# Feed-forward output stages: 12 of 22 inner k tiles by seven block products in place of eight

## The reference

```
def swiglu(x, w_in, w_out):                      # w_in 1024 x 5632, w_out 2816 x 1024
    gate, up = jnp.split(x @ w_in, 2, axis=-1)
    return (jax.nn.silu(gate) * up) @ w_out
x <- LN1(alpha*x + 0.5*swiglu_1(x))              # stages f1i (input), f1o (output)
x <- LN2(alpha*x + W_out[concat(PoolMix(u), RWKV7(z))])   # stages z, wo
h  = alpha*x + 0.5*swiglu_2(x)                   # stages f2i, f2o
x <- LN3(h + sigmoid(h W_g + b_g) * (p W_ple))   # stage gp
```

## Time and profile before

| | us |
|---|---|
| median of 3 runs (2641.80 to 2646.03) | 2642.49 |
| span of the profiled execution (the page shows no time around it) | 2641.4 |
| PE busy | 2536.3 (96%) |
| DVE / ACT / POOL busy | 1686.9 / 933.7 / 1585.4 |
| matmuls | 27280 |
| read from and written to HBM | 186.95 MB, 3.12 MB |

### The profile page before, as it was taken

How to read it: one execution, slowest core, us unless ns; L and a number is a source line. 1 busy time by engine, 2 the same in 40 slices (tenths; PEclk the granted TensorE clock), 3 DMA queues, 4 the chain that set the end, 5 groups by cost and what they waited for, 6 DMA issues and landing times. The chain is left out here.

```text
span 2641.4 us, 65842 instructions
## 1 busy us (share of the span) xinstructions
PE 2536.3 (96%) x27280; PEld 2444.1 (93%) x27280; DVE 1686.9 (64%) x2492; ACT 933.7 (35%) x1942; POOL 1585.4 (60%) x1319
## 2 busy tenths in 40 slices
PE   8999999989999999999999999999899999999997
PEld 8999999978888999999999999999788799999996
DVE  5866318756663889931598982377566659898124
ACT  3444004445531345410245530144445214553002
POOL 6555666734325677666767766667343266776665
PEclk9999999999998999999999999999899999999998
DMA  4222332200001232223222323321000022332322
GB/s 155 96 98 81 91 105 73 81 2 5 4 21 42 81 104 98 94 84 95 86 96 98 103 85 88 96 81 57 4 4 5 20 73 89 102 102 82 88 87 79
DMA packets 81901, 193.70 MB, mean 73 GB/s; under 512 B 13680, under 2 KB 14064, under 8 KB 81648
## 3 DMA queue, kind: packets, MB, share of 16 engines
q1 hardware_dynamic: 78192, 187.07, 22.1%
q10 hardware_dynamic: 3456, 3.02, 0.4%
HBM read 186.95 MB, written 3.12 MB: 72 GB/s over the span
## 5 line engine op out<-in xcount | busy, mean ns | idle before, releaser
L874 PE MATMUL ps<-xa,w_hi 128*128 128x272 f32 x2208 | 583.4, 289 | 4.2 <-DVE w_lo L1800 2.7
L874 PE MATMUL ps<-xa,w_lo 128*128 128x272 f32 x1932 | 560.6, 290 | 0.0
L874 PE MATMUL ps<-xb,w_hi 128*128 128x272 f32 x1656 | 478.9, 289 | 0.0
L665 POOL TENSOR_SCALAR w_hi<-w_raw 128x1024 fp32r<-128x1024 f32 (+2 forms) x217 | 232.0, 1069 | 366.0 <-PE ps L760 359.0
L874 PEld LDWEIGHTS ps<-xa,w_hi 128*128 128x128 f32 x2208 | 399.2, 189 | 6.5 <-DVE w_lo L1800 3.3
L874 PEld LDWEIGHTS ps<-xa,w_lo 128*128 128x128 f32 x1932 | 364.2, 189 | 0.0
L669 POOL TENSOR_TENSOR w_lo<-w_raw,w_hi 128x640 fp32r<-128x640 f32 (+2 forms) x217 | 352.1, 1623 | 0.0
L874 PEld LDWEIGHTS ps<-xb,w_hi 128*128 128x128 f32 x1656 | 312.7, 189 | 0.0
L760 PE MATMUL ps<-hh,w_hi 128*128 128x272 f32 x1472 | 304.9, 288 | 5.6 <-DVE hl L1828 5.4
L760 PE MATMUL ps<-hh,w_lo 128*128 128x272 f32 x1472 | 302.7, 288 | 0.0
L760 PE MATMUL ps<-hl,w_hi 128*128 128x272 f32 x1472 | 302.3, 287 | 0.0
(11 more groups left out here) (364 smaller groups left out, 5698.2 us busy)
## 6 DMA issues: line engine op xcount, KB each, us to landing
w_raw<-in_wz SPq DMA_DIRECT2D x44, 512.0 KB, 3.3
w_odd<-in_w1i SPq DMA_DIRECT2D x72, 256.0 KB, 3.0
w_odd<-in_w2i SPq DMA_DIRECT2D x72, 256.0 KB, 3.1
w_raw<-in_w1i SPq DMA_DIRECT2D x68, 256.0 KB, 2.9
w_raw<-in_w2i SPq DMA_DIRECT2D x64, 256.0 KB, 3.0
w_raw<-in_w1o SPq DMA_DIRECT2D x32, 448.0 KB, 3.3
w_raw<-in_w2o SPq DMA_DIRECT2D x32, 448.0 KB, 3.3
w_raw<-in_w2i SPq DMA_DIRECT2D x20, 512.0 KB, 3.4
```

What stands on the lines that cost most here:

```text
L665: pool.tensor_scalar(w_hi[k][:, 0:nk, :], w_raw[k][:, 0:nk, :], 1.0, 0.0, ALU.mult, ALU.add).then_inc(w_hi_done, 1)
L874: mm = pe.matmul(ps[:, bank(site, b, j), 0:HT], w, x, start=(j in FRESH and k + i == 0), stop=(k == 3 and i == 2), skip_group_check=True)
```

## The change

In each output stage 10 of the 22 k tiles (rows 0 to 9, those that are rounded within `seven`) remain plain, now in slots of 5. The other 12 form two k halves of 6 (`LOW_ROW`, `HIGH_ROW`). With the pairs of output tiles and the token halves they make 2 x 2 blocks, and for each of four pairs (`blocks(b)`, b = 0 to 3) seven products (t = 0 to 6) of 18 matmuls are made: two groups g of three k tiles, three matmuls each.

PE does plain(0), blocks(0), blocks(1), plain(1), blocks(2), plain(2), blocks(3), plain(3). Products are accumulated in shared banks: DVE adds a bank's state to `y` after some of the products (`add`, 272 columns), and PE waits for that (`o_part`) before it adds the next product into the bank. `add_pair` (544 columns) adds the two banks of a whole tile; `summed` is the addition to `ysum` (f1o alone) and `rounded` the low part for the next stage, now after the last block.

The activation side has, per stage, 8 differences of hidden rows (`hidden_sum`, DVE, 816 columns), 14 roundings (`hidden_high`, ACT) and 14 low parts (`hidden_rest`, DVE); the former rounding of rows 10 to 21 is gone. The weight side has, per block, 8 sums or differences of 384 columns (`sums_12`, `sums_3`, `sums_4`) by DVE into `s1_out` and `s2_out`, which lie in SBUF; 8 roundings by ACT (`sum_high`); 8 low parts by DVE (`low`); and 6 items (t = 0, 1, 6, two groups each) that POOL splits. The items use the same `w_hi` and `w_lo` as the plain parts, four entries of three tiles in turn (`item`); an entry is free when the product two before is done (`item_free`), or when the third or fourth plain part is.

The block weights are loaded by four DMAs of 6 k tiles per block, in the SP queue between the plain parts. The embedding input of gp is loaded into another buffer, and two semaphores are merged; neither changes the number of its operations.

```diff
-PHASES = [("f1i", FT, [8, 8]), ("f1o", 4, [8, 7, 7, 8, 7, 7]), ("z", NZ // 2, [8, 8]), ("wo", 4, [8, 8]),
-          ("f2i", FT, [8, 8]), ("f2o", 4, [8, 7, 7, 8, 7, 7]), ("gp", 4, [5, 5, 5, 5])]
+PHASES = [("f1i", FT, [8, 8]), ("f1o", 4, [5, 5, 5, 5]), ("z", NZ // 2, [8, 8]), ("wo", 4, [8, 8]),
+          ("f2i", FT, [8, 8]), ("f2o", 4, [5, 5, 5, 5]), ("gp", 4, [5, 5, 5, 5])]
...
+PLAIN_ROWS, PAIRS = 10, 6
+LOW_ROW, HIGH_ROW = PLAIN_ROWS, PLAIN_ROWS + PAIRS
+A11, A12, A21, A22 = range(4)
+PLAIN_A = {0: (A11, 0), 1: (A12, 2), 6: (A22, 4)}
+SUM_A = {2: 0, 3: 2, 4: 4, 5: 6}
+PARTS = (0, 6, 10, 14, 18)
...
+        def item(b, t, g):
+            if b == 3:
+                slot, tile = ((1, 0), (1, 3), (0, 5), (0, 0))[2 * (t % 2) + g]
+            else:
+                slot, tile = ((0, 0), (0, 3), (1, 5), (1, 0))[2 * ((t + (b == 1)) % 2) + g]
+            return [w[slot][:, tile:tile + 3, :] for w in (w_hi, w_lo)]
+        def item_free(eng, s, b, t, g):
+            l, name = OUT_SITES[s]
+            i = 14 * (4 * s + b) + 2 * t + g
+            if t >= 2 or b == 1:
+                eng.wait_ge(a_mm, i - 3)
+            else:
+                if b:
+                    eng.wait_ge(a_mm, 14 * (4 * s + b))
+                eng.wait_ge(slot_used, used_count(l, name, 4 * max(b - 1, 0) + 2 + (t == 1 and g == 1)))
...
+                def blocks(b):
+                    n = 4 * s + b
+                    if b == 0:
+                        sp.wait_ge(v_plain, (v0 + ns) * 3)
+                        sp.wait_ge(v_add, (v0 + ns) * 4)
+                        sp.wait_ge(v_sum, (v0 + ns) * 3)
+                    for a in (A21, A11, A12, A22):
...
+                        sp.dma_start(a_raw[a][:, :, :], src[l * 8 + 2 * b + (a in (A21, A22)), :, r:r + PAIRS, :]).then_inc(a_loaded[a], 16)
+                plain(0, 0)
+                plain(0, 1)
+                blocks(0)
+                plain(0, 2)
+                plain(0, 3)
+                plain(1, 0)
+                plain(1, 1)
...
+                def blocks(b):
+                    n = 4 * s + b
+                    for t, (a, o) in PLAIN_A.items():
+                        pool.wait_ge(a_loaded[a], (n + 1) * 16)
+                        for g in range(2):
+                            hi, lo = item(b, t, g)
+                            src = a_raw[a][:, 3 * g:3 * g + 3, :]
+                            item_free(pool, s, b, t, g)
+                            pool.tensor_scalar(hi, src, 1.0, 0.0, ALU.mult, ALU.add).then_inc(a_hi, 1)
+                            pool.wait_ge(a_hi, n * 6 + o + g + 1)
+                            pool.tensor_tensor(lo, src, hi.bitcast(F32), ALU.subtract).then_inc(a_plain, 1)
+                for b in range(4):
+                    if b:
+                        blocks(b)
+                    for i in range(4):
+                        plain(b, i)
+                    if b == 0:
+                        blocks(b)
...
+                def blocks(b):
+                    n = 4 * s + b
+                    part = s * 18 + PARTS[b]
+                    if b >= 2:
+                        for k in range(2):
+                            pe.wait_ge(tile_out[k], out_count(l, name, b - 2))
+                    for t in range(7):
+                        bank = BANKS[b][(2, 0, 2, 3, 2, 1, 2)[t]]
+                        if b == 1 and t == 1:
+                            pe.wait_ge(o_part, s * 18 + 2)
+                        if t in (2, 4, 6):
+                            pe.wait_ge(o_part, part + {2: 1, 4: 3 if b == 0 else 2, 6: 6 if b == 0 else 4}[t])
+                        if t == 5 and b:
+                            pe.wait_ge(o_part, part + 3)
+                        for g in range(2):
+                            if t in PLAIN_A:
+                                pe.wait_ge(a_plain, n * 6 + PLAIN_A[t][1] + g + 1)
+                            else:
+                                pe.wait_ge(as_lo, n * 8 + SUM_A[t] + g + 1)
+                            if b == 0:
+                                pe.wait_ge(hx_ready, s * 14 + 2 * t + g + 1)
+                            hi, lo = item(b, t, g)
+                            for i in range(3):
+                                for q, (w, x) in enumerate(((hi, h_hi(t, g)), (hi, h_lo(t, g)), (lo, h_hi(t, g)))):
+                                    fresh = (g, i, q) == (0, 0, 0) and (t in (0, 3) or t == 1 and b > 0)
+                                    mm = pe.matmul(ps[:, bank, 0:HT], w[:, i, :], x[:, i, :], start=fresh,
+                                                   stop=(g, i, q) == (1, 2, 2), skip_group_check=True)
+                            mm.then_inc(a_mm, 1)
...
+                    else:
+                        hidden_sum(s, 3, 0)
+                        hidden_sum(s, 3, 1)
                     value_second(b)
                     if b + 1 < ns:
                         sums_2(b + 1)
+                    else:
+                        hidden_sum(s, 2, 0)
                     gate_second(b)
                     between(b, 1)
+                hidden_sum(s, 4, 0)
+                hidden_sum(s, 6, 0)
...
+            def hidden_sum(s, j, g):
+                l, name = OUT_SITES[s]
+                site = l, name[:2] + "i"
+                end = V0[site] + SEVEN[site]
+                low = [rows_of(hlf, LOW_ROW, g, h) for h in range(2)]
+                high = [rows_of(hlf, HIGH_ROW, g, h) for h in range(2)]
+                free, made = {3: (3, 0), 2: (4, (1, 2)[g]), 4: (6, 0), 6: (6, (4, 7)[g])}[j]
+                dve.wait_ge(v_mm, (end - 1) * 7 + free)
+                dve.wait_ge(v_row, end - (PAIRS if j == 3 else 3 - 3 * g))
+                if made:
+                    dve.wait_ge(hx_sum, s * 8 + made)
+                a, b = {3: (low[1], low[0]), 2: (high[1], h_sum(3, g)), 4: (high[1], low[1]), 6: (high[0], h_sum(2, g))}[j]
+                dve.tensor_tensor(h_sum(j, g), a, b, ALU.subtract).then_inc(hx_sum, 1)
+            def hidden_rest(s, j, g):
+                dve.wait_ge(hx_hi, s * 14 + 2 * j + g + 1)
+                dve.wait_ge(hx_sum, s * 8 + 8)
+                dve.tensor_tensor(h_lo(j, g), h_sum(j, g), h_hi(j, g).bitcast(F32), ALU.subtract).then_inc(hx_ready, 1)
+            def outputs(s, inst, parts):
+                l, name = OUT_SITES[s]
+                site = l, name[:2] + "i"
+                end = V0[site] + SEVEN[site]
+                blk_of = lambda t, g: t[:, 3 * g:3 * g + 3, :]
+                def sums_12(b):
+                    n = 4 * s + b
+                    dve.wait_ge(a_loaded[A21], (n + 1) * 16)
+                    dve.wait_ge(a_loaded[A22], (n + 1) * 16)
+                    for g in range(2):
+                        dve.tensor_tensor(s1_out[:, g, :, :], blk_of(a_raw[A21], g), blk_of(a_raw[A22], g), ALU.add).then_inc(as_add, 1)
+                    dve.wait_ge(a_loaded[A11], (n + 1) * 16)
+                    for g in range(2):
+                        dve.wait_ge(as_add, n * 8 + g + 1)
+                        dve.tensor_tensor(s2_out[g], s1_out[:, g, :, :], blk_of(a_raw[A11], g), ALU.subtract).then_inc(as_add, 1)
...
+                hidden_sum(s, 2, 1)
+                hidden_sum(s, 4, 1)
+                hidden_sum(s, 6, 1)
+                dve.wait_ge(v_plain, end * 3)
+                for j in (0, 1):
+                    for g in range(2):
+                        hidden_rest(s, j, g)
+                sums_12(0)
+                for j in (2, 3, 4, 5):
+                    for g in range(2):
+                        hidden_rest(s, j, g)
+                if parts is None:
+                    dve.memset(ysum[:, :], 0.0).then_inc(sum_ready, 1)
+                dve.wait_ge(ax_ready, inst * 8 + 8)
+                low(0, 2)
+                add(0, 0, 4, 0, 0, 0).then_inc(o_part, 1)
+                dve.wait_ge(slot_used, used_count(l, name, 3))
+                add_pair(1, 2).then_inc(o_part, 1)
+                for g in range(2):
+                    hidden_rest(s, 6, g)
+                low(0, 3)
+                sums_3(0)
+                add(0, 2, 4, 0, 1, 2).then_inc(o_part, 1)
...
+                for b in range(1, 4):
+                    a, c = BANKS[b][2:4]
+                    sums_12(b)
+                    summed(2 * b - 2)
+                    summed(2 * b - 1)
+                    low(b, 2)
+                    add(b, 0, a, 0, 0, 0).then_inc(o_part, 1)
...
+                    dve.wait_ge(slot_used, used_count(l, name, 4 * b + 3))
+                    add_pair(2 * b + 1, BANKS[b][4]).then_inc(tile_out[1], 1)
```

More of the change, by code:

```diff
@@ L725, in _ @@
                         split(l, name, 0, ks, 1)
-                    ahead = (l, name[:2] + "i") in SEVEN and name in ("f1o", "f2o")
-                    if ahead:
-                        split(l, name, 0, ks, 0, 1)
-                        pool.wait_ge(v_mm, (V0[l, name[:2] + "i"] + SEVEN[l, name[:2] + "i"]) * 7)
-                        split(l, name, 0, ks, 1)
+                    if (l, name) in OUT_SITES:
```

(14 more changed lines are left out.)

290 lines of the change are left out of this document (241 added, 49 removed).

## The result

The changed kernel takes 2698.13 us (median of 4, 2696.59 to 2699.99) against 2643.23 (4 runs): a ratio of 1.0209, 95% interval 1.0195 to 1.0224. It is slower by 55 us; 2691 was forecast. S is again a stage's first matmul.

What follows compares the result with a forecast made beforehand. PE alone was taken to bound the output stages. With matmuls and waits summed, f1o takes 149.3 us and f2o 142.3; four stages 583.2 against 534.6, +48.6 on 2642.5, giving 2691; range 2618 to 2720.

Steps and rivals of the forecast that it cites:

- Matmuls: Each output stage: 984 matmuls instead of 1056, at least 123.8 us against 133.65, 9.8 less, 39.4 in four stages.
- the sign that PE's busy time would fall by 36: Whole kernel: 288 fewer matmuls lower PE's busy time by about 36 us, whatever the time does.
- Block 0: Start of each output stage: third product waits for DVE's first add, 11.3 us late; 13.9 lost per stage with later waits.
- the turns: Block 0: DVE operations with two SBUF inputs and POOL's splits alternate on SBUF, so their times nearly add up.
- the factor 0.92: Block 0: share of summed DVE and POOL times; (18.0 + 14.2) x 0.92 + 1.3 starts the third product at S + 30.9.
- a sign against itself that POOL ends the waits: PE's waits in the stages: forecast wrong if POOL or a DMA ends them, rather than a DVE operation.
- Blocks 1 to 3: Third products wait for DVE's chain behind add_pair: 3.7 us lost per f2o stage, 8.2 per f1o, plus 2.5 for clock.
- The 0.3 that each plain part was to start late: Plain parts behind a block: POOL splits them only after the sixth product; 0.9 us lost per stage.
- Costed at nothing: Output stages: ACT's some 30 us stay hidden; DMA and plain part 2's late load, some 2 us, hidden behind block 0's wait.
- Rival 1: Output stages: turns cost little and PE stays the bound; 2614 us, or 2603 without the small losses; chance 0.18.
- rival 2: Output stages: block 0 pays in full, blocks 1 to 3 do not; +20 us, 2662; chance 0.16.
- rival 3: Output stages: every wait at its upper bound; +97 us, 2739; chance 0.04.

Runs made afterwards that it cites:

- experiment 10: Kernel with 4, 5 and 6 and each stage's first pair made without block products, then the orders of items, DVE work and loads mended; 2628.19 us, ratio 0.9933 to before.
- the repeat: The changed kernel, unaltered, profiled and timed again; 2692.69 us, ratio 1.0179 to the kernel before.
- Experiments 1: Changed kernel with POOL splitting only 8 of each 128 weight columns of block 0's plain parts 1 to 3 and early items; 2652.48 us, ratio 1.0036 to before.
- 2: Changed kernel with 12 DVE low parts per stage set to zero by memset instead of subtracted; 2661.33 us, ratio 1.0069 to the kernel before.
- 7: All edits: changed kernel with 3, 4, 5 and 6, plain part 2's load issued first and the ysum memset late; 2659.56 us, ratio 1.0072 to before.
- 8: Same edits as 7, but the low parts of hidden blocks 3 to 5 stay ahead of the first add; 2661.10 us, ratio 1.0075 to before.
- 3: Changed kernel with six of block 0's low parts moved in DVE's queue behind the first add; 2686.32 us, ratio 1.0170 to the kernel before.
- 6: Changed kernel with ACT instead of POOL rounding weights of block 0's plain parts 1 to 3 and first four items; 2688.22 us, ratio 1.0174 to before.
- 4: Changed kernel with f1o's two ysum additions in blocks 1 to 3 moved behind the first add; 2679.95 us, ratio 1.0132 to the kernel before.
- 5: As 4, with the first four weight sums of blocks 2 and 3 moved ahead of the last add_pair; 2670.11 us, ratio 1.0115 to the kernel before.

## Why the prediction came out as it did

**Matmuls: right.** 288 fewer. The last pair in experiment 10, without a wait, takes 31.1 us; four such are 124.4 against 123.8 forecast. The gain of 9.8 per stage was there to be had (9.2 by this row). Wrong was the sign that PE's busy time would fall by 36: it fell by 4.5 within the stages and rose by 4.5 over the whole (in the repeat it fell by 3.0). Some 20 of the missing us in the stages are matmuls at half clock; the rest was not traced. The 115.8 ns taken from the Trainium skill (TensorE: Matmul & The Clock Gate, Back-to-back issue gap) are given there for an isolated matmul, not for a stream of weight loads and matmuls as here. The rows' 125.1 and 126.5 ns decide.

**Block 0: right in place, cause and size, wrong in which engine ends the waits.** The third product starts at S + 29.9 to 30.4 in the four stages, forecast S + 30.9; block 1 starts 12.2 to 12.4 us behind its ideal, forecast 13.9. Experiments 1 and 2 show the turns, and the factor 0.92 foretold the starts in 7 and 8 within 1 us. In 3 and 6 the expectations were reckoned otherwise and missed by 4 to 5 and by about 2 us; the sum, taken afterwards, comes within 1.2 us there. By the exclusive lock in full (the Trainium skill, SBUF — State Buffer, Who interferes with whom) the product would have started at S + 33.5; the measurement lies at 0.89 to 0.90 of the sum. The prediction named as a sign against itself that POOL ends the waits, and in part it did: ahead of the third product POOL's splits ended 5.3 to 6.1 us of PE's idle time in each stage, DVE's `add` 0.3 to 3.1. The work of both engines added up as forecast, but PE met it as several waits on POOL and one on DVE, not as one long wait on DVE. Another detail was off: the 816-column operations have medians of 1.30 to 1.56 us, not near 1.7.

**Blocks 1 to 3: right for f1o, too small for f2o.** The idle time at the third products of blocks 2 and 3 is 1.08 us in f2o (forecast 1.1) and 2.23 in f1o (2.6). Counted from start to start, these products come 1.5 and 2.6 late, and the three blocks lose 5.4 to 5.6 us a stage in f2o (forecast 3.7) and 10.4 to 11.8 in f1o (8.2, and 2.5 for the clock). Block 1 also waits 0.4 and 0.6 on POOL's items in both. The 0.3 that each plain part was to start late did not show: 15.0 us from its first matmul to the next block.

**Stages.** f1o 147.9 and 146.7 (149.3 forecast), f2o 141.7 and 141.5 (142.3): 577.8 against 583.2. They lie 5 to 6 apart, about 7 was forecast. In both, block 0 was put too high: its third product 0.5 to 1.0 earlier than forecast, and behind it 1.4 to 1.9 lost in place of 2.6. In f2o that and the 0.9 for the plain parts were some 2.5 too much, and the later blocks 1.8 too little, so the stage came out closer than its terms. The whole came out 7 us above the forecast all the same, since the 13.6 us outside the stages, most of them the clock of that execution, stood in no term. That it lies within 0.3% of the measurement is thus partly luck.

**Costed at nothing.** ACT's 30 to 32 us stayed hidden. The late load of plain part 2, for which POOL stood still for 1.9 us in the second stage, mostly did too, as block 0 was late anyway: with the load issued first (8) the third product came no earlier than without that (6), S + 27.5 against 27.6. With POOL thin the load shows as a wait of 0.9.

**Rival 1** (turns cost little) fell by experiments 1 and 2; rival 2 (later blocks cost nothing) by 4 and 5; rival 3 (every wait at its bound, 2739) by the time itself.

## What to carry to other kernels

Fewer matmuls pay only where the engines that prepare them have the time before they are due; add up their work up to the first due point, with the turns that two engines take on SBUF, not over the stage. Here, having DVE's work due 33 us after the stage's start instead of 15 turned +9 us in the four stages (all edits) into -7, and with that kernel's queues mended into -20, at a price of 72 matmuls. And an idle time's releaser names only the last of several late engines: moving DVE's work alone (experiment 3) or POOL's alone (6) uncovered the other.

## What was not expected

PE's clock behind the recurrences was granted at 0.50 for 20.5 us in some executions and not in others, worth about 8 us each time, in the trace of the kernel before as in those of the changed ones. What decides it was not found. Executions of the kernel before spread over 2633 to 2654 us on one chip, with mean clocks of 0.990 down to 0.982. A difference of 10 us between two single traces of this kernel can be that alone.
